# The opening of a two-layer encoder kernel: four weight units multiply rows that are only scaled

## The reference, cut to what matters

```python
for l in range(DEPTH):                       # 2 layers, x is 512 tokens x 1024
    mod = silu(c) @ ada_w[l] + ada_b[l]      # 9 vectors of 1024, shift sh and scale sc among them
    h = rmsnorm(x, g) * (1 + sc1) + sh1
    x = x + 0.5 * g1 * swiglu(h)             # gate, up = split(h @ w_in); (silu(gate) * up) @ w_out
    ...                                      # token mixing, then a second swiglu like the first
```

## Time and profile before

| | |
|---|---|
| median of 3 runs (lowest to highest) | 2324.29 us (2323.8 to 2324.96) |
| the profiled execution: time, span | 2327.99 us, 2326.3 us |
| busy in the span: PE, DVE, ACT, POOL | 2302.5, 1284.4, 852.4, 113.7 us |
| mean granted clock of TensorE, full speed being 1 | 0.995 |
| DMA over the span | 138 GB/s read and written |

### The profile page before, as it was taken

How to read it: one execution, slowest core, us unless ns; L and a number is a source line. 1 busy time by engine, 2 the same in 40 slices (tenths; PEclk the granted TensorE clock), 3 DMA queues, 4 the chain that set the end, 5 groups by cost and what they waited for, 6 DMA issues and landing times.

```text
span 2326.3 us, 37275 instructions
## 1 busy us (share of the span) xinstructions
PE 2302.5 (99%) x14356; PEld 1872.5 (80%) x14356; DVE 1284.4 (55%) x1860; ACT 852.4 (37%) x1277; POOL 113.7 (5%) x220
## 2 busy tenths in 40 slices
PE   8999999999999999999999999999999999999998
PEld 6888888777778888888878888887777788888887
DVE  4554556786457664433475545577756576443334
ACT  5231224542455543223342212345225555331222
POOL 1000000020000000000000000101000000000000
PEclk8999999999999999999999999999999999999999
DMA  8564563353334344433245645623332353453231
GB/s 317 193 211 154 178 204 125 100 145 96 99 114 151 112 136 153 145 99 104 95 135 189 209 138 196 212 96 106 116 102 91 118 178 95 148 170 101 90 113 60
DMA packets 96182, 325.38 MB, mean 140 GB/s; under 512 B 12904, under 2 KB 15624, under 8 KB 95040
## 3 DMA queue, kind: packets, MB, share of 16 engines
q1 hardware_dynamic: 57936, 215.56, 28.5%
q0 software_dynamic: 23760, 82.48, 11.3%
q10 hardware_dynamic: 14368, 25.70, 3.1%
HBM read 306.34 MB, written 14.73 MB: 138 GB/s over the span
## 4 chain that ended last, share of the span: by engine, by line
PE 93%; DVE 3%; ACT 1%; issue 1%; DMA 1%; SPq 0%; DVEq 0%; POOL 0%; ACTq 0%; POOLq 0%
PE PS L566 81%; PE PS L1187 4%; PE PS L895 1%; DVE h L1898 1%; PE PS L581 0%; PE PS L1135 0%; PE PS L1161 0%; PE PS L604 0%; DVE wl L1652 0%; DVE t_buf L1925 0%; DMA ada<-in_ada_first_dram 0%; PE PS L1170 0%; PE PS L886 0%; ACT wh L1264 0%; DMA ada_raw<-in_ada_w_dram 0%
## 5 line engine op out<-in xcount | busy, mean ns | idle before, releaser
L1652 DVE TENSOR_TENSOR wl<-raw,wh 128x1024 fp32r<-128x1024 f32 (+2 forms) x360 | 466.1, 1295 | 775.0 <-ACT wh L1264 774.3
L566 PE MATMUL PS<-uh,wh 128*128 128x512 f32 x2176 | 860.8, 396 | 3.5 <-DVE wl L1652 2.1
L566 PE MATMUL PS<-ul,wh 128*128 128x512 f32 x2176 | 847.9, 390 | 0.0
L566 PE MATMUL PS<-uh,wl 128*128 128x512 f32 x2176 | 847.9, 390 | 0.0
L1264 ACT ACTIVATE wh<-raw 128x1024 fp32r<-128x1024 f32 (+2 forms) x360 | 402.3, 1118 | 869.2 <-PE PS L566 851.4
L566 PEld LDWEIGHTS PS<-uh,wh 128*128 128x128 f32 x2176 | 408.3, 188 | 99.9 <-issue 7.4
L566 PEld LDWEIGHTS PS<-uh,wl 128*128 128x128 f32 x2176 | 408.5, 188 | 86.5
L566 PEld LDWEIGHTS PS<-ul,wh 128*128 128x128 f32 x2176 | 408.8, 188 | 80.7
L566 PE MATMUL PS<-hh,wh 128*128 128x512 f32 x726 | 283.1, 390 | 0.0
L566 PE MATMUL PS<-hl,wh 128*128 128x512 f32 x726 | 282.5, 389 | 0.0
L566 PE MATMUL PS<-hh,wl 128*128 128x512 f32 x726 | 282.5, 389 | 0.0
(11 more groups left out here) (302 smaller groups left out, 1663.5 us busy)
## 6 DMA issues: line engine op xcount, KB each, us to landing
raw<-in_ffn_in_dram SPq DMA_DIRECT2D x176, 512.0 KB, 3.6
ada_raw<-in_ada_w_dram POOLq DMA_DIRECT2D x144, 512.0 KB, 3.9
raw<-in_mix_in_dram SPq DMA_DIRECT2D x88, 512.0 KB, 3.6
raw<-in_ffn_out_dram SPq DMA_DIRECT2D x32, 768.0 KB, 4.3
raw<-in_ffn_out_dram SPq DMA_DIRECT2D x32, 640.0 KB, 3.9
g_in<-gates_dram ACTq DMA_DIRECT2D x48, 256.0 KB, 3.1
ada<-in_ada_first_dram SPq DMA_DIRECT2D x8, 1024.0 KB, 16.5
raw<-in_mix_up_dram SPq DMA_DIRECT2D x16, 512.0 KB, 3.6
```

The lines of the kernel that those rows point to most:

```text
L566: mm = e.matmul(PS[:, bank, :], w[:, j % 2, k * P:(k + 1) * P], v[:, k, :], start=(k == 0 and w is wh and v is xh), stop=(k == K - 1 and w ...
L1652: TTo(wl[:, j % 2, 0:K * P], raw[:, j, 0:K * P], wh[:, j % 2, 0:K * P], ALU.subtract)\
```

## The change

The first stage gets the split formula for all four of its first units. A lot now holds the sums of two rows, and the four lots with the scales come first, then the four with the shifts. Units 0 and 1 multiply rows x * scale as lots 0 to 3 arrive; the sums of the lots stand between their rows and those of unit 2. After lot 7 PE does the shift sums of all four raw units (64 small matmuls in place of 32), then unit 3. Meanwhile DVE and ACT make the fully modulated rows, into the same uh and ul, row by row as unit 3 lets go of them; unit 4 is the first to use them. The reload of raw waits for the shift sums. POOL asks for the first two ada rows before the tables, which wait for unit 5's arrival. Core of the diff; the host packs `ada_first` to match:

```diff
-WAKE = 32
+WAKE = (16, 14, 7)
...
+                            tokens(0)
+                            ada_lot(0)
...
+                            for j in range(2):
                                 load(0, 0, j, a[name + "_in"][j], KD)
+                            tokens(1)
+                            ada_lot(1)
...
+                            for j in range(2, 4):
+                                tokens(j)
+                                ada_lot(j)
+                            for j in range(2, 4):
+                                load(0, 0, j, a[name + "_in"][j], KD)
+                            for lot in range(4, ADA_LOTS):
+                                ada_lot(lot)
+                            e.dma_start(cond[:, :], a["c"].broadcast_to([P, KD * P])).then_inc(cond_in.sem, 16)
...
+                first_sums(0)
+                wake(WAKE[1])
+                rows(0, range(0, 2))
+                rows(1, range(0, 2))
+                first_sums(1)
+                wake(WAKE[2])
+                rows(0, range(2, 4))
+                first_sums(2)
+                rows(1, range(2, 4))
+                rows(0, range(4, 6))
+                first_sums(3)
+                rows(1, range(4, 6))
...
+                rows(0, range(6, 8))
+                rows(1, range(6, 8))
+                first_sums(4)
+                rows(2, range(0, 2))
...
+                spread()
+                first_sums(5)
+                rows(2, range(2, 4))
+                first_sums(6)
+                rows(2, range(4, 6))
+                first_sums(7)
+                rows(2, range(6, 8))
+                e.wait_ge(first_mods.sem, ADA_LOTS // 2)
+                shift_sums(4)
+                rows(3, range(0, 8))
...
+                        e.wait_ge(silu_done.sem, silu_done.at(0, 1))
+                        unit(0, RAW, 0, KD, 0, uh, ul, shifted_there)
+                        for j in range(1, 4):
+                            in_unit(1, j)
...
+            e.wait_ge(rstd_mm.sem, 1)
+            e.activation(gate_hold[:, :], PS[:, 6, :], ACT.Copy).then_inc(first_root.sem, 1)
+            split(0, 0, 0, 3, KD)
...
+            shifted_row(0)
+            first_silu(0)
+            shifted_row(1)
+            split(0, 1, 0, 0, KD)
+            for k in range(2, 6):
+                shifted_row(k)
+            first_hh(0)
+            shifted_row(6)
+            shifted_row(7)
+            first_silu(1)
+            split(0, 1, 0, 1, KD)
+            first_hh(1)
...
+            def first_hl(p):
+                e.wait_ge(hh_done.sem, p + 1)
+                TTo(hl[:, p, :], h32[:, p, :], hh[:, p, :], ALU.subtract).then_inc(hl_done.sem, 1)
+                for b in range(2):
+                    ada_main(0, p, b)
...
+            first_sums(7)
+            first_times_root(0, 0, silu_s[:, 0, :])
+            first_times_root(1, 2, h32[:, 0, :])
+            for k in range(4, 6):
+                normed(k)
+            shift_columns(0, 0)
+            normed(6)
+            shifted_lo(0)
+            normed(7)
+            shifted_lo(1)
+            first_h(0)
+            split(0, 1, 0, 0, KD)
+            for k in range(2, 5):
+                shifted_lo(k)
+            first_times_root(2, 1, silu_s[:, 1, :])
+            shifted_lo(5)
+            shifted_lo(6)
+            shifted_lo(7)
+            first_times_root(3, 3, h32[:, 1, :])
+            split(0, 1, 0, 1, KD)
...
+            first_hl(0)
+            first_h(1)
+            first_hl(1)
```

More of the change, by code:

```diff
@@ L41 @@
 UNITS = 180
-LAG = 3
-WAKE = 32
+WAKE = (16, 14, 7)
 SUB = 60
@@ L644, in first_units @@
                 e.wait_ge(mods_done.sem, mods_done.at(l, s + 1))
[L645 to L651, removed]
+                shift_sums(2)
                 unit(l, n + 1, 1, KD, banks[1], yh, yl, None, range(4, KD), True)
@@ L1214, in _ @@
             e.wait_ge(mean_in.sem, 16)
[L1215 to L1218, removed]
+            wake(WAKE[0])
+            e.wait_ge(cond_done.sem, 1)
             for l in range(DEPTH):
@@ L1324, in use_in @@
                             e.activation(dst, h32[:, j // 2, :], ACT.Copy).then_inc(hh_done.sem, 1)
-                    apart = half == 0 and (l, s) != (0, 0)
-                    steps(e, l, first, 2 * F, KD, F, split, use_in, False, (lambda: None) if apart else None)
+                    opened = (l, s, half) == (0, 0, 0)
+                    apart = half == 0 and not opened
+                    steps(e, l, first, 2 * F, KD, F, split, use_in, False, (lambda: None) if apart else None, opened)
                     first += 2 * F
@@ new lines, in first_hh @@
+            def first_hh(p):
+                e.wait_ge(h_done.sem, h_done.at(0, p + 1))
+                e.activation(hh[:, p, :], h32[:, p, :], ACT.Copy).then_inc(hh_done.sem, 1)
+            squares(range(0, 2))
+            split(0, 0, 0, 0, KD)
+            e.wait_ge(consts_in.sem, 16 * 4)
+            scaled_row(0)
+            scaled_row(1)
+            split(0, 0, 0, 1, KD)
+            squares(range(2, 4))
+            scaled_row(2)
+            scaled_row(3)
+            squares(range(4, 8))
@@ L1611, in _ @@
+            for k in range(4, KD):
+                scaled_row(k)
+            split(0, 0, 0, 2, KD)
             e.activation(warm[:, 0:1], eps[:, 0:1], ACT.Sqrt)
             root(0, 0)
[L1614 to L1623, removed]
@@ new lines, in first_sums, with first_lo @@
+                for part in range(2):
+                    v = d + part
+                    last = STT(out=scale_eff[:, v:v + 1], in0=ada_sum[:, KD + v:KD + v + 1], scalar=norm_g[:, 0, v:v + 1],
+                               in1=scale_0[:, v:v + 1], op0=ALU.mult, op1=ALU.add)
+                last.then_inc(first_scale.sem, 1)
+            def first_lo(k):
+                e.wait_ge(yh_done.sem, k + 1)
+                e.wait_ge(first_scale.sem, k // 2 + 1)
+                STT(out=ul[:, k, :], in0=x[:, k, :], scalar=scale_eff[:, k:k + 1], in1=uh[:, k, :], op0=ALU.mult,
+                    op1=ALU.subtract).then_inc(yl_done.sem, 1)
@@ new lines, in _ @@
+            normed(1)
+            split(0, 0, 0, 3, KD)
+            first_sums(6)
+            for k in range(2, 4):
+                normed(k)
[3 more added lines that the diff above has]
+            for k in range(4, 6):
+                normed(k)
+            shift_columns(0, 0)
[5 more added lines that the diff above has]
+            split(0, 1, 0, 0, KD)
```

260 lines of the change are left out of this document (151 added, 109 removed).

## The result

| | before | after |
|---|---|---|
| median of 22 runs each, run in turn (lowest to highest) | 2324.93 us (2322.5 to 2328.55) | 2328.52 us (2326.94 to 2330.07) |
| the profiled execution: time, span | 2327.99, 2326.3 us | 2327.79, 2326.1 us |

The ratio is 1.0015, with an interval of 1.0008 to 1.0021: the changed kernel takes 3.6 us more. The interval is clear of 1, and the difference lies inside the 4.65 us that were called "no change". Spans can't be set side by side here; the same point of the work in both kernels can.

The account below looks back on a forecast made before the run. PE's own order was taken to bound the kernel, with idle time only in the opening. Unit 6's lead of -1.2 us plus +2.2, +1.2 and +1.0 made +3.2 us: 2327.5 us, range 2321 to 2333.

Parts of the forecast that it names:

- no change: Whole kernel: 0.2% of its time, 4.65 us, about what a measurement can tell from no change; forecast chance 0.52.
- two open terms: Opening: "issue" holes on the path, +1.2 us, and an early fall of the clock, +1.0 us.
- the lead: Opening: changed kernel ends unit 3 at 51.2 us against 59.5 before, 8.3 us ahead.
- unit 6 against before (70.4): Start of unit 6: 69.2 us against 70.4 in the kernel before, -1.2 us.
- the clock behind unit 6's hole: After the hole before unit 6: clock falls to 0.50, costing 1.7 to 3 us, taken as +2.2.
- "issue" holes on the path: PE's instruction stream up to unit 6: one of two earlier holes recurs, +1.2 us, bounds 0 and 3.4.
- the clock early on: First rows, 11 to 25 us: clock may fall to half, 0 to +5 us, taken as +1.
- DVE's list: Between shift sums and unit 6: most of 8.2 us of added DVE work gives the lead back in three steps.
- Unit 4's feed: Raw's reload after the shift sums: issue 0.4, landing 3.6, splits 1.0 and 1.2; 6.6 us used, unit 4 at 52.4.
- The slower one: Whole kernel: early clock stays low, or both "issue" holes and a late clock rise; first case 2331.5 us; chance 0.36.
- The faster one: Up to unit 6: ada rows in time, shift sums sooner, no clock fall; -3 to -8 us, middle 2319; chance 0.12.
- its second half: Faster rival: shift sums stand where lot 7's arrival lets them, about 39 us; everything moves up by up to 4.8 us.

Follow-up runs that it names:

- experiment 1: Changed kernel with the four ada-row reductions before unit 6's split moved behind the splits of units 6 and 7; 2328.13 us, 1.0011 against the kernel before.
- experiment 2: Changed kernel with the first six pairs of reductions dealt out, four behind splits of units 6, 8, 10, 12; 2322.21 us, 0.9989 against the kernel before.
- experiment 3: Changed kernel with two more DVE operations of 1.15 us between the reductions and unit 6's split; 2330.36 us, 1.0025 against the kernel before.
- experiment 4: Changed kernel with POOL asking for its first two ada rows only when unit 4's weights have landed; 2328.29 us, 1.0011 against the kernel before.
- experiment 7: Changed kernel with experiment 4's and experiment 5's edits, and loads of units 5 to 7 held until unit 4's landed; 2326.69 us, 1.0009 against the kernel before.
- experiment 8: Changed kernel with the edits of experiment 2 and experiment 7 together; 2320.56 us, 0.9983 against the kernel before.
- experiment 5: Changed kernel with raw buffers of units 0 and 1 let go after half of the shift matmuls; 2328.14 us, 1.0013 against the kernel before.
- experiment 9: Changed kernel without the 14 and 7 constant matmuls behind the sums of lots 0 and 1; 2332.40 us, 1.003 against the kernel before.
- experiment 10: Kernel before with 24 matmuls of a constant added in its own early PE holes; 2322.79 us, 0.999 against the kernel before.

## Why the prediction was right

The time was forecast at 2327.5 us, it is 2328.52; +3.2 us were worked out, +3.6 came. The path was right, the size came out by luck: 2.2 of the 3.2 us were two open terms that did not occur, and the lead was smaller by about as much. The terms:

| | predicted | measured |
|---|---|---|
| first product, us | 12.9 | 14.13 |
| rows 2 and 3 of the first units start | 19.9 | 21.05 |
| shift sums: start, how long | 43.8, 2.0 | 46.00, 1.97 |
| unit 4 starts, hole before it | 52.4, 1.2 | 55.64, 2.2 |
| unit 5 | 58.8, 0.9 | 61.99, 0.8 |
| unit 6 | 69.2, 5.0 | 72.44, 4.9 |
| unit 6 against before (70.4) | -1.2 | +2.0 |
| the clock behind unit 6's hole | +2.2 | +1.5 |
| "issue" holes on the path | +1.2 | 0 |
| the clock early on | +1.0 | 0 |
| sum | +3.2 | +3.5 |

- **The mechanism held.** A lead in the first rows is given back by DVE's list: three holes before units 4, 5 and 6, with 0.8 and 4.9 us for the last two where 0.9 and 5.0 were worked out, the DVE split as releaser and a reload of an ada buffer ahead of it. Experiments 1, 2 and 3 show it by moving, removing and lengthening the hole. The wait was that for the second reloaded buffer, asked for 1.1 us behind the first and landed in 4.51 us, and not that for the first (3.8 us), for which the sum had 4.4; the length came out the same.
- **The lead was sized too large, by 2.2 us at the shift sums.** This is the step that failed, in two parts. The first product came 1.2 us later: unit 0's weights, for whose landing the sum had no term, were there only at 11.0 us, and ACT's and DVE's splits of them end at 13.3. From rows 2 and 3 on PE took 24.95 us to the shift sums and not 23.9. The holes weren't it (1.1 and 0.3 us before the products at 26.27 and 31.48 us, where 2.0 were given), nor the token sums and the root's spread (1.7 us, 2.1 given), but the rows: the chain has two rows between two lots' sums at 1.59 us (44.41 to 46.00), where 2 x 0.68 were counted. Over the nine stretches of rows between sums this comes to 1.8 us. No stretch "issue" of the size in the earlier trace rows stands on the path there. The prediction kept +1.2 and +1.0 apart as open terms for such stretches and for the early clock; their size made up for this error, and that was luck, since their causes did not occur.
- **Unit 4's feed was 1.0 us too cheap.** A landing of 3.6 us was taken, near the 3.4 that the earlier trace rows has as the least; it took 4.91. (The terms listed for the feed, 0.4 + 3.6 + 1.0 + 1.2, make 6.2 us; 6.6 was used, 7.7 came.) The median of that group, 6.4, was the warning. Two megabytes of raw and one of ada rows were asked for at nearly the same time, and with POOL's part later it took 4.11 (experiment 4). The Trainium skill (DMA: Bandwidth & Descriptors, "Issuing engines are not separate DMA queues") says that transfers started by different engines end up on the same 16 DMA engines and interleave; these two runs agree. It is not the whole cause: with no other load asked for beside it, the same load took 3.6 us in experiment 7 and 5.03 in experiment 8. The Trainium skill's formula (same page, "Anatomy of one DMA"), which that page gives for transfers issued by GpSimd, makes an estimate of 3.2 us for 512 KB; unit 4's load is issued by SyncE and took 3.6 to 5.8 us here, the ada rows that GpSimd issues took 3.8 and 4.51 in the changed kernel, and the measurement decides.
- **The clock.** Behind the hole of 4.9 us it was at 1.2 GHz for 3.1 us, which costs 1.5; 2.2 was taken, 1.7 was named for a stretch of 3.4. The cost is not a constant: behind the same hole in experiments 3, 4, 5, 7 and 9 it was 1.6, 2.3, 2.6, 1.8 and 2.4 us. In the first rows it did not fall, and experiment 9 shows that the constant's matmuls are the reason: without them it falls there, the shift sums stand 1.4 us later, and the kernel loses 3.9 us in all. The rule of the Trainium skill that the prediction weighed (TensorE: Matmul & The Clock Gate, "Why this matters for your kernels"), that gaps between products cost the clock, agrees with this trace in both places; the hole of 2.2 us before unit 4 cost nothing in the changed kernel and 1.6 us in experiment 1.
- **A slip without effect.** The splits of the earlier trace rows are those of units 6 and 7, not 7 and 8. Their distance, which is all that was used, is the same.
- **The rivals.** The slower one needed the early clock to fall, which it did not. The faster one needed the ada rows in time and the shift sums sooner. Experiments 2 and 8 take the reductions out of the way (2322.2 and 2320.6 us); the shift sums stood at 46.0 and 45.8 us in them, so its second half was never met. What decides is the place of four reductions, 4.6 us of work and two reloads, in DVE's order: PE came to the end of unit 3 6.1 us ahead of the kernel before (53.4 against 59.5), and the holes before units 4, 5 and 6 took 7.9 us.

What stays open: why the landing of raw's reload varied between kernels with the same edit (5.03 us in experiment 8, 3.6 in 7), and what the gaps called "issue" are that stand at 522.88 and 1826.40 us in the kernel before's profiled execution and at 1668.21 us in experiment 9's, while the changed kernel has none at these places. The first two are about the 3 us by which that execution lies above its median. How long the clock stays at half behind unit 6's hole also differs between executions, so a lead read at one point of one profile and the difference of the medians can part by about 1 us, as in experiments 4 and 5.

## What to carry to other kernels

A weight split that stands behind slower work in an engine's order waits for all of it, so work whose buffer must be reloaded between two uses belongs behind the split and spread out, not only moved behind it (experiment 1 gained nothing): the same change with its reductions spread is 2.4 us faster than the kernel before, with unit 4's load sooner 4.1 us, and as made it is 3.6 us slower. Size a transfer by the median of its landings, not the least. Look at the granted clock of an opening before rebuilding it: with 24 small matmuls in its holes the kernel before was 2.3 us faster by the medians (interval 0.2 to 4.4), of which the profile shows 0.85 us in the opening.

## What the runs showed of the hardware that was not expected

- Holes of one length cost the clock in one kernel and not in another: behind 2.2 us before unit 4 it stayed at 1.00 in the changed kernel, behind 2.2 us in experiment 1 and 2.05 us in experiment 2 it fell, to 0.69 over 55 to 60 us.
- Products of 128x512 that stand between runs of short ones are dearer: two rows of three take 1.59 us there, 2 x 0.68 us inside a long run. The 0.2 us lie at the two changes (first distance 0.33 us, last 0.33, in place of 0.23).
- The load of unit 4's weights, 512 KB, took 3.6 to 5.8 us to land. One that was asked for 1.22 us sooner landed 0.3 us sooner (5.83 against 4.91 us, experiment 5).
- The reload of an ada buffer behind a reduction took 0.7 us until POOL had issued it. On the chains shown above it took 4.5 to 5.0 us to land; over all such reloads between 60 and 110 us in experiments 1, 2, 3, 7 and 8 it took 3.5 to 7.2 us. In experiment 1 two reloads on the path start 6.73 us apart (69.07 and 75.80), the pace of a pair of reductions.
- The kernel before itself spreads over 2322.5 to 2328.55 us, more than the changed one does (2326.94 to 2330.07). With its early holes filled it spreads over 2321.97 to 2323.44 us (11 runs, experiment 10); why was not found.
